# Mixers of a hybrid RWKV-7, retention and Mamba-2 decoder step: Mamba's scratch in the weight ring, RWKV ahead of its v tiles, and the projection in half slots

## The reference, cut to what matters

```python
c = rmsnorm(x) @ w_in
ya, sh, Sa = rwkv7_mixer(c[..., :COLS_A], ...)                 # 6 heads: r, k, v, two low-rank inputs, gate
yb, Sb     = retention_mixer(c[..., COLS_A:COLS_A+COLS_B], ...) # 4 heads: q, k, v, gate
yc, cv, hc = mamba2_mixer(c[..., COLS_A+COLS_B:], ...)          # 6 heads: z, convolved x, B, C, and dt
x = x + concatenate([ya, yb, yc]) @ w_out
# RWKV-7, token by token (S is value x key):
sa = S @ (-kk);  S = S * w + sa (kk * a)^T + v k^T;  y = S @ r
```

## Time and profile before

| | |
|---|---|
| median of 3 runs | 1687.14 us (1686.18 to 1692.51) |
| the profiled execution | 1686.05 us |
| its span, first to last instruction | 1684.3 us |
| TensorE matmul busy | 1484.4 us (88%) |
| VectorE, ScalarE, GpSimd busy | 926.5, 738.9, 109.5 us |
| mean granted TensorE clock | 0.865 |

### The profile page before, as it was taken

How to read it: one execution, slowest core, us unless ns; L and a number is a source line. 1 busy time by engine, 2 the same in 40 slices (tenths; PEclk the granted TensorE clock), 3 DMA queues, 4 the chain that set the end, 5 groups by cost and what they waited for, 6 DMA issues and landing times.

```text
span 1684.3 us, 27530 instructions
## 1 busy us (share of the span) xinstructions
PE 1484.4 (88%) x10644; PEld 1283.3 (76%) x10644; DVE 926.5 (55%) x1453; ACT 738.9 (44%) x1108; POOL 109.5 (7%) x144
## 2 busy tenths in 40 slices
PE   4899899886699999899989988566899999999996
PEld 3897778765699999788877876466587788778874
DVE  3534454434544344455355443453488888888985
ACT  4522233112333343362223321232378777877774
POOL 0001010111000000000011020100000000000000
PEclk8877889655899999988889975586699999999998
DMA  7211111103344444332110110230389778877971
GB/s 274 94 52 51 45 39 34 48 0 138 101 142 150 138 145 142 112 101 74 58 50 1 51 68 1 112 121 13 111 301 330 288 290 325 306 287 290 348 276 69
DMA packets 62055, 234.83 MB, mean 139 GB/s; under 512 B 7057, under 2 KB 7153, under 8 KB 61073
## 3 DMA queue, kind: packets, MB, share of 16 engines
q1 hardware_dynamic: 59328, 217.61, 37.0%
q0 software_dynamic: 2496, 13.71, 2.1%
q10 hardware_dynamic: 144, 2.28, 0.3%
HBM read 225.48 MB, written 8.09 MB: 139 GB/s over the span
## 4 chain that ended last, share of the span: by engine, by line
PE 54%; issue 32%; DVE 9%; ACT 3%; POOL 1%; DMA 1%; POOLq 0%; ACTq 0%; DVEq 0%
PE bank L459 11%; PE bank L460 10%; PE bank L461 10%; PE bank L453 8%; PE bank L723 1%; PE bank L473 1%; PE bank L602 1%; ACT whi L1100 1%; PE bank L858 1%; PE bank L600 1%; PE bank L588 1%; PE bank L811 1%; PE bank L570 1%; DMA x<-in_x 1%; DVE htmp L1512 1%
## 5 line engine op out<-in xcount | busy, mean ns | idle before, releaser
L1497 DVE TENSOR_TENSOR wlo<-wraw,whi 128x1024 fp32r<-128x1024 f32 x410 | 501.5, 1226 | 350.9 <-ACT whi L1100 339.0
L1100 ACT ACTIVATE whi<-wraw 128x1024 fp32r<-128x1024 f32 x410 | 433.0, 1059 | 386.0 <-PE bank L461 294.8
L459 PE MATMUL bank<-hh,whi 128*128 128x320 f32 x968 | 335.4, 347 | 58.3 <-DVE hl L1517 36.5
L460 PE MATMUL bank<-hl,whi 128*128 128x320 f32 x968 | 321.6, 332 | 0.0
L461 PE MATMUL bank<-hh,wlo 128*128 128x320 f32 x968 | 320.1, 331 | 0.0
L459 PEld LDWEIGHTS bank<-hh,whi 128*128 128x128 f32 x968 | 202.9, 210 | 69.7 <-issue 40.9
L460 PEld LDWEIGHTS bank<-hl,whi 128*128 128x128 f32 x968 | 203.8, 211 | 1.4 <-issue 0.5
L461 PEld LDWEIGHTS bank<-hh,wlo 128*128 128x128 f32 x968 | 202.0, 209 | 0.0
L1018 PE MATMUL bank<-whi,hh 128*128 128x512 f32 (+1 forms) x384 | 149.0, 388 | 1.1 <-DVE place L2043 1.1
L1020 PE MATMUL bank<-wlo,hh 128*128 128x512 f32 (+1 forms) x384 | 144.3, 376 | 0.0
L1019 PE MATMUL bank<-whi,hl 128*128 128x512 f32 (+1 forms) x384 | 144.0, 375 | 0.0
(11 more groups left out here) (380 smaller groups left out, 2156.5 us busy)
## 6 DMA issues: line engine op xcount, KB each, us to landing
wraw<-in_w SPq DMA_DIRECT2D x410, 512.0 KB, 5.0
smb<-in_s_ssm POOLq DMA_DIRECT2D x2, 1536.0 KB, 8.0
out_o_ssm<-smb POOLq DMA_DIRECT2D x2, 1536.0 KB, 5.6
cst<-in_consts ACTq DMA_DIRECT2D x1, 2225.0 KB, 12.4
srw<-in_s_rwkv POOLq DMA_DIRECT2D x2, 768.0 KB, 6.7
out_o_rwkv<-srw POOLq DMA_DIRECT2D x2, 768.0 KB, 4.4
x<-in_x SPq DMA_DIRECT2D x1, 1280.0 KB, 12.2
out_y<-x SPq DMA_DIRECT2D x1, 1280.0 KB, 4.5
```

The costliest lines, as they stand in the source:

```text
L459: mm(out, hi, rh, start=first, stop=False)
L460: mm(out, hi, rl, start=False, stop=False)
L1100: af(whi[:, ring % HI, :], wraw[:, POS[ring], :], ACT.Copy).then_inc(S("slot_hi"), 1)
L1497: tt(wlo[:, POS[ring], :], wraw[:, POS[ring], :], whi[:, ring % HI, :].bitcast(F32), ALU.subtract).then_inc(S("slot_split"), 1)
```

## The change

Six things are changed together; no arithmetic of the result is.

1. The order of tiles: RWKV's v tiles come after r, k and the first two of retention's q tiles, dt early, and z ahead of retention's gate. The block order of each mixer stays.
2. A slot can be cut in two halves of 12 matmuls. After 11 early slots, `gaps` places a half in each planned wait of blocks 2, 0 and 1 of RWKV.
3. Mamba and retention use banks 0 and 1; Mamba's scratch lies in six places of the ring, so that the projection has 5 places (`RIN`) while it runs and 2 output slots (`KEEP`) can be loaded ahead, not 4. `whi` stays free. Given states of retention and Mamba take the place of RWKV's, one after the other, each loaded when the one before is stored. Retention's third block stands before the last slots, and Mamba runs while block 1 of RWKV does.
4. Of `prep`, the products kp, rho and the bonus by v are GpSimd's, and X2 lies behind Dx.
5. `sample_states` makes one product of 2 x 8 columns for both operands, alternating between heads on partitions 0 to 63 and 64 to 127; Mamba's block 2 alternates likewise.
6. Mamba's results are kept in `cZ` and copied to `hh` when the last slot has been used.

```diff
-Z_TILE, X_TILE = A_TILES + B_TILES, A_TILES + B_TILES + TC
-ORDER = [9, 10, 3, 4, 5, 0, 1, 2, 6, 7, 8] + [WIN - 1] + list(range(A_TILES, A_TILES + 6)) \
-    + list(range(X_TILE, X_TILE + XT)) + [A_TILES + 6, A_TILES + 7] + list(range(Z_TILE, Z_TILE + TC))
+Q_TILE, Z_TILE, X_TILE = A_TILES, A_TILES + B_TILES, A_TILES + B_TILES + TC
+ORDER = [9, 10, 3, 4, 5, WIN - 1, 0, Q_TILE, 1, 2, Q_TILE + 1, 6, 7, 8] + list(range(Q_TILE + 2, Q_TILE + 6)) \
+    + list(range(X_TILE, X_TILE + XT)) + list(range(Z_TILE, Z_TILE + TC)) + [Q_TILE + 6, Q_TILE + 7]
 NA, NI = A_TILES, WIN - A_TILES
+N_EARLY = ORDER.index(6)
+A_CNT = [sum(t < NA for t in ORDER[:j + 1]) for j in range(WIN)]
+I_CNT = [sum(t >= NA for t in ORDER[:j + 1]) for j in range(WIN)]
+def tile_in(l, tile):
+    return NI * l + I_CNT[ORDER.index(tile)]
 
 
...
-KEEP = 4
+RIN, KEEP = 5, 2
...
-POS = [(g - max(s for s in [0] + G_OUT if s <= g)) % RAW for g in range(N_SLOTS)]
+FIRST = [max(s for s in G_IN + G_OUT if s <= g) for g in range(N_SLOTS)]
+POS = [(KT + (g - FIRST[g]) % RIN) % RAW if FIRST[g] in G_IN else (g - FIRST[g]) % RAW for g in range(N_SLOTS)]
...
 LEVELS = [6, 6, 3]
 CHUNKS_OF = [2, 2, 1]
-DN = [7 + 4.5 * j if j < NA else 57 + 6.6 * (j - NA) for j in range(WIN)]
-DQ = [0.45 if j < NA else 0.8 for j in range(WIN)]
-DE = [DN[j] + 8 * DQ[j] for j in range(WIN)]
-END = DE[-1]
-LEV = 7.0
+LEV = 6.2
 CHS = 8.0
-RW_AT = [98.0, 158.0, 58.0]
+RW_AT = [92.0, 148.0, 56.0]
 RW_CH = [RW_AT[b] + 8 + LEV * (LEVELS[b] - 1) for b in range(3)]
 RW_FIN = [RW_CH[b] + CHS * CHUNKS_OF[b] for b in range(3)]
 RW_NEW = RW_CH[2] + 5
-TOK_AT = [11.0, 14.0, 1.5]
-RT_AT = [110.0, 135.0, END + 8]
-MB_AT = [END + 3, END + 57, END + 28]
-DT_AT = RW_AT[2] + 13
+def gaps(b, levels, chunks):
+    at = [RW_AT[b] + w for w in (1.0, 2.5, 4.3, 5.6)]
+    at += [RW_AT[b] + 8 + LEV * q + w for q in range(levels) for w in (0.5, 2.9)]
+    return at + [RW_CH[b] + w for w in chunks]
+HALVES = [h for j in range(N_EARLY) for h in (7 + 4.2 * j, 8.9 + 4.2 * j)] \
+    + gaps(2, 2, (0.6, 2.7, 5.0, 7.0)) + gaps(0, 5, (0.6, 2.7, 8.6, 10.7)) + gaps(1, 2, ())
+DN = HALVES[0::2]
+DH = HALVES[1::2]
+DE = [h + 1.9 for h in DH]
+END = DE[-1]
+TOK_AT = [11.0, 14.0, 12.3]
+TOK_OF = [(0, 1, 2), (0, 1, 2), (1, 2, 0)]
+RT_AT = [98.0, 115.0, 132.0]
+MB_AT = [152.0, 200.0, 173.0]
+DT_AT = RW_AT[2] + 8
...
-        srw = sb("srw", [P, TA, NSEQ, HD])
-        X1, X2, aa, Pi, kp = (sb(n, [P, TA, T]) for n in ("X1", "X2", "aa", "Pi", "kp"))
+        X1, aa, Pi, kp = (sb(n, [P, TA, T]) for n in ("X1", "aa", "Pi", "kp"))
...
+        srw_at = top[0]
+        srw = sb("srw", [P, TA, NSEQ, HD])
         rwx_at = top[0]
         rwx = sb("rwx", [HD, 2, NSEQ, P])
         vx = sb("vx", [HD, HB, NSEQ, HD], offset=rwx_at)
+        srt = sb("srt", [P, TB, NSEQ, HD], offset=srw_at)
+        smb = sb("smb", [P, 2, NSEQ, 3, HD], offset=srw_at)
+        assert srw_at + 2 * NSEQ * 3 * HD * 4 <= top[0]
         qk_at = top[0]
         qk = sb("qk", [P, 4, P])
...
                     for k in range(KT):
-                        if k and j < NA:
-                            yield DN[j] + k * DQ[j]
+                        if k == KT // 2:
+                            yield DH[j]
...
-                yield RW_AT[2] + 1
+                yield RW_AT[2] + 1.2
                 pe.wait_ge(S("srw_in"), 16 * (l + 1))
                 pe.wait_ge(S("pre_act"), pre(l, "g_done"))
-                for bk, src in ((0, X2), (1, Dx[:, 3:6, :])):
-                    for h in range(HA):
-                        if h % 2 == 0:
-                            yield RW_AT[2] + 1 + 4 * bk + h
-                        p = slice(64 * (h % 2), 64 * (h % 2) + 64)
-                        for s in range(NSEQ):
-                            t8 = slice(SEQ + s * STEP, SEQ + (s + 1) * STEP)
-                            m = mm(B[bk][p, (h // 2) * CH + s * STEP:(h // 2) * CH + (s + 1) * STEP],
-                                   srw[p, h // 2, s, :], src[p, h // 2, t8], start=True, stop=True)
-                    m.then_inc(S("rw_S0"), 1)
+                pe.wait_ge(S("pre_pool"), pre(l, "rho_done"))
+                for t in range(TA):
+                    yield RW_AT[2] + (1.2, 2.7, 4.5)[t]
+                    for s in range(NSEQ):
+                        t8 = slice(SEQ + s * STEP, SEQ + (s + 1) * STEP)
+                        for o in range(2):
+                            p = slice(64 * o, 64 * o + 64)
+                            out = B[0][p, 0:2 * TA * CH].rearrange("p (z t c) -> p z t c", z=2, t=TA)
+                            m = mm(out[:, :, t, s * STEP:(s + 1) * STEP], srw[p, t, s, :],
+                                   Dx[p, 3 + t:A_TILES + t + 1:A_TILES - 3, t8], start=True, stop=True)
+                m.then_inc(S("rw_S0"), 1)
 
...
-                for h in range(HC):
-                    p = slice(64 * (h % 2), 64 * (h % 2) + 64)
-                    lo = (h // 2) * P
-                    mx(B[6][p, lo:lo + n], xdt[0:n, h, :], seg[0:n, h, 0:n], True, False)
-                    if b == 2:
-                        for s in range(NSEQ):
-                            m = mx(B[6][p, lo + s * STEP:lo + (s + 1) * STEP], smb[:, h // 3, s, h % 3, :],
+                for t in range(TC):
+                    two = [(h, slice(64 * (h % 2), 64 * (h % 2) + 64)) for h in (2 * t, 2 * t + 1)]
+                    for h, p in two:
+                        mx(B[0][p, t * P:t * P + n], xdt[0:n, h, :], seg[0:n, h, 0:n], True, False)
+                    if b < 2:
+                        for h, p in two:
+                            m = mx(B[0][p, t * P:t * P + n], smb_p[:, h * HD:(h + 1) * HD], cde[:, h, 0:n], False, True)
+                        continue
+                    for s in range(NSEQ):
+                        for h, p in two:
+                            m = mx(B[0][p, t * P + s * STEP:t * P + (s + 1) * STEP], smb[:, h // 3, s, h % 3, :],
                                    cde[:, h, s * STEP:(s + 1) * STEP], False, s == NSEQ - 1)
-                    else:
-                        m = mx(B[6][p, lo:lo + n], smb_p[:, h * HD:(h + 1) * HD], cde[:, h, 0:n], False, True)
                 m.then_inc(S("mb_y"), 1)
...
                 act.wait_ge(S("mb_y3"), it)
-                af(hh[:, TA + TB:KT, c0:c0 + n], yz[:, :, 0:n], ACT.Copy).then_inc(S("mb_yh"), 1)
+                act.wait_ge(S("slot_used"), G_OUT[l])
+                af(hh[:, TA + TB:KT, c0:c0 + n], cZ[:, :, c0:c0 + n], ACT.Copy).then_inc(S("mb_yh"), 1)
...
-                act.wait_ge(S("mb_done"), 3 * (l + 1))
                 for g in range(G_OUT[l], G_OUT[l] + HI):
-                    hi(g, g, ROUND[g])
+                    hi_ahead(g - HI)
...
+            def prep(l):
+                yield 37.8
+                gp.wait_ge(S("pre_act"), pre(l, "t1_done"))
+                tt(kp[:, :, :], kp[:, :, :], Dx[:, 3:6, :], ALU.mult).then_inc(S("pre_pool"), 1)
+                yield DE[ORDER.index(2)] + 1.6
+                gp.wait_ge(S("pre_pool"), pre(l, "kp_done"))
+                gp.wait_ge(S("pre_dve"), pre(l, "kk_done"))
+                gp.wait_ge(S("a_read"), NA * l + A_CNT[ORDER.index(2)])
+                for t in range(TA):
+                    for p_, r_, rho in zip(pe_parts(1), parts(Dx[:, 0:3, :]), parts(Dx[:, 3:6, :])):
+                        m = tt(rho[:, t], p_[:, t], r_[:, t], ALU.mult)
+                m.then_inc(S("pre_pool"), 1)
+                yield RW_AT[0] - 8
+                gp.wait_ge(S("pre_act"), pre(l, "g_done"))
+                gp.wait_ge(S("a_read"), NA * (l + 1))
+                tt(X1[:, :, :], X1[:, :, :], Dx[:, 6:9, :], ALU.mult).then_inc(S("pre_pool"), 1)
...
-                        gp.wait_ge(S("rw_tok"), 9 * l + 1)
+                        gp.wait_ge(S("rw_tok"), 9 * l + 3)
                     else:
                         gp.wait_ge(S("rw_ds"), 3 * l + t)
                     tt(rwx[:, 1, :, :], rep(tok[0:CH, 0, t, :], NSEQ), over(C("seq", rows=slice(0, CH)), P),
                        ALU.mult).then_inc(S("rw_xv"), 1)
                 yield RW_NEW + 16
                 gp.wait_ge(S("rw_sS"), 3 * (l + 1))
-                out(o_rw[l], srw[:, :, :, :])
+                gp.dma_start(o_rw[l], srw[:, :, :, :]).then_inc(S("ring_out"), 16)
+                yield RW_NEW + 24
+                gp.wait_ge(S("ring_out"), 16 * (3 * l + 1))
+                gp.dma_start(srt[:, :, :, :], s_rt[l]).then_inc(S("srt_in"), 16)
...
+                    yield s0 + 22
+                    gp.wait_ge(S("ring_out"), 16 * (3 * l + 2))
+                    gp.dma_start(smb[:, :, :, :, :], s_mb[l]).then_inc(S("smb_in"), 16)
```

More of the change, by code:

```diff
@@ L870, in mamba @@
                 for q in range(3):
-                    m = mm(B[7][:, 0:n], C("ones"), ysq[:, q, 0:n], start=(q == 0), stop=(q == 2))
+                    m = mm(B[1][:, 0:n], C("ones"), ysq[:, q, 0:n], start=(q == 0), stop=(q == 2))
                 m.then_inc(S("mb_ms"), 1)
@@ L1230, in tokens @@
```

(6 more changed lines are left out.)

206 lines of the change are left out of this document (97 added, 109 removed).

## The result

The changed kernel takes 1697.49 us (median of 4 runs, 1696.39 to 1698.66) against 1686.98 us for the kernel before (4 runs, 1686.18 to 1692.51): ratio 1.0085, 95% interval 1.0044 to 1.0127. It is slower, by about 10 us, where 1628 us was forecast, in a range from 1587 to 1668. The difference is small beside the spread of the kernel before: in the 45 runs of it that accompany the experiments, on three chips, it took 1672.70 to 1695.74 us. The four runs of the changed kernel lie above all of them.

The account below looks back on a forecast made before the run. The mixers were taken as bound by TensorE in program order, through matmul time, idle gaps and clock. Terms -9, -1, -11.5, -4.5 and -3 gave -29 us a layer, -58 in all: 1628 us, range 1587 to 1668.

Parts of the forecast that it names:

- C: TensorE's idle gaps in the mixers: half slots placed in the waits save a net 11.5 us a layer, bounds 3 to 16.
- The waits only move: Rival, chance 0.2: slot conversions in VectorE's in-order queue delay the chain, so saved gaps reopen elsewhere; -8.5 a layer, 1669 us.
- D: Clock in RWKV block 2: half slots from the start raise it to 0.80 and 0.83, -4.5 us a layer, bounds 0 to -10.
- Slower (0.06): Rival, chance 0.06: halves of 1.9 us between small products are too thin to hold the clock up; 1707 us.
- A: RWKV sample states: 96 records on alternating array quarters take about 5.5 us, not 14.5; -9 us a layer, bounds -7.2 and -10.9.
- B: Mamba's sample outputs, 96 records of 11.2 us alternated by column halves: -1 us a layer, between 0 and -5.6.
- E: Retention 2 and most of Mamba 0 move out of the low-clock tail: -3 us a layer, bounds -1 and -6.
- Mamba's gaps: Waits for the decay (4.6 us) and GpSimd's spread (2.9 us) shrink by 2 and 2.9; under 3 us together afterwards.
- The new states: 64x512 products lose their filler and await GpSimd's 2.9 us spread twice: +2 us a layer, two gaps of 2 to 3.
- GpSimd's pieces: Preparation products moved to GpSimd: rho may delay VectorE, +1.5 us a layer, bound +3; the other two pieces 0.
- Ring depth and landings: Projection ring cut from 11 to 5 places and only two output slots fetched ahead: costs nothing.

Follow-up runs that it names:

- lo_behind: The changed kernel with VectorE's low-half conversion (wlo) of the slots in the chains planned behind the update of TM and TT: 1651.07 us, ratio 0.9794.
- whole_mended: both_orders with each projection slot issued whole at the place of its first half: 1640.14 us, ratio 0.9740.
- both_orders: The changed kernel with VectorE's slot conversion behind the update of TM and TT, and the splits of finished outputs 20 us later: 1640.02 us, ratio 0.9731.
- serial: both_orders with RWKV's and Mamba's sample products issued one array half after the other, as in the kernel before: 1676.05 us, ratio 0.9952.
- best: both_orders plus Mamba's first-block finish and retention's gate behind Wm, and two half slots moved between the new states' products: 1619.79 us, ratio 0.9603.

## Why the prediction was wrong

**The step that failed** is C, "What changes is where they stand: ... as half slots of about 1.9 us, one in each wait", which priced what a half slot covers and left out what each slot brings along on the other engines: a conversion on ScalarE and one on VectorE, tied to that slot's end and placed in the same in-order queues as the chain's pieces. The gaps that C meant did shrink: all idle time other than that for TT and Wm went from 48.9 - 6.5 = 42.4 to 54.1 - 23.2 = 30.9 us, -11.5 a layer where -14.9 + 3.5 was forecast, Wm's 2.5 among them. But the waits for TT and Wm grew by 16.7 us. Net +5.3 instead of -11.5.

The mechanism stood among the rivals, as "The waits only move", but was priced as C and D nothing, 1669 us. That was its second error: nothing bounds such a wait by the gap that was there before, and with six of them, of up to 3.1 us, the chain lost more than it had to gain. lo_behind shows it: 0.4 us in the plan were worth 46 us. Its chance of 0.2 was too low for a mechanism whose condition could be read beforehand: the place of each wlo against TM and TT in VectorE's order, and the line that makes whi wait for the slot three back. The rival "Slower (0.06)" had the outcome, but for another reason, halves too thin for the clock; whole_mended and both_orders, 1640 us each, speak against that one.

**D**, clock in block 2, 0.80 and -4.5 us: it stayed at 0.75, and over the two mixers the clock fell. Busy time went from 334.2 to 331.5 in layer 0 and from 324.0 to 328.2 in layer 1, though A and B took about 16.3 us out of each: 13.8 and 20.3 us went to slower matmuls, where D and E had forecast -7.5. It's not a second cause but the first one again, since with the two orders mended the same sum is -7.2 and +5.3, about nothing. For block 2 alone D then comes true: its stage, 72.4 us in the changed kernel where near 60 was forecast, is 61.3 us at 0.85 in both_orders and 58.6 at 0.92 in lo_behind. But it is 62.4 at 0.86 in whole_mended too, so the halves are not what does it. Over the whole mixer the half slots did not raise the clock against whole ones: whole_mended has 0.79 and 0.78, both_orders 0.81 and 0.80, for the same time. The Trainium skill describes such a loss (TensorE: Matmul & The Clock Gate, the section on its second failure mode: in a kernel with 512 columns in bf16, short idle gaps between groups of matmuls make the clock go up and down). The runs here agree: in lo_behind 17.7 us of matmul time went with 9.2 us of waits in layer 0, and 9.9 with 10.6 in layer 1.

**A**, -9 a layer: -10.9 and -10.5, at its best bound: 96 records in 3.6 us are 37.5 ns each, the 38 of the levels in the earlier trace rows. **B**, -1 with bound -5.6: it is the bound, 96 records in 5.6 us instead of 11.2. Products with all 128 rows of weights overlap here when consecutive ones go to different column halves. Together they were worth 36 us in serial, which takes them away. So the mechanism of A was right and its size nearly; B was mis-sized by 4.6 us a layer.

**E**: the tail went from 121.0 to 93.0 us (97 forecast). What was gained there is in the rows, but not to be told apart from the loss in block 0.

**The other points.** Mamba's gaps: L899 waits for nothing now (2.9 before), L858 3.0 us instead of 4.6. The new states: the two waits of 2 to 3 us are there, 2.66 and 2.37, as the +2 had it; filling them again is worth 13 to 16 us in both layers, three to four times that term; in the profiled executions 6 us of it are idle time and 7 matmul time. GpSimd's pieces delay nothing: block 2 starts behind 1.23 us of issue. Ring depth and landings: no wait of TensorE, ScalarE or VectorE in layer 0's mixer names a DMA, so nothing, as costed.

**The sum**, a layer, forecast and measured: A and B -10 and -16.3; idle -11.5 and +5.3; clock, with E, -7.5 and +17; in all -29 and +6. With the orders mended: -16.3, -6.2 and -1, in all -23.5, or 47 us for two layers, against 58 forecast. So even with the queue mended idle time and clock give 7.2 us of the 19 that C, D and E had, and what A and B bring beyond their terms, 6.3 us, hides half of what is missing. C's idle time is reached only in best, where all four places are mended: 35.7 us are left in each mixer, 13 and 14 less than before.

## What to carry to other kernels

A filler put into a wait isn't only its own length: list every instruction that it triggers on the other engines, find in each in-order queue what stands behind them, and ask whether they become ready before or after the piece that the chain needs. When such a conversion is late, put it behind the chain's piece, or convert one slot earlier, rather than take the filler away. And where TensorE's clock moves with its waits, a wait can cost more than its length; here nearly two microseconds of matmul time went with each microsecond of wait in one layer, and about one in the other.
